# Gated delta rule of a two-part block: chunks of 128 tokens in place of 64, with waits for one token tile

## The chip, the cores and the metric

The kernel runs as one program on one core of one Trainium2 chip. The metric is the device time of one execution in microseconds (us). TensorE is called PE below, VectorE DVE, ScalarE ACT, GpSimd POOL and SyncE SP.

## The reference

The reference computes two small models in a row on 256 tokens of width 1024, all in float32. The first has two layers; its second layer is the gated delta rule, which the change is about. The second model has two layers of mixing and an expert layer each (16 experts, three 1024 x 1024 matrices per expert).

```
def gated_delta_rule(q, k, v, g, beta):
    c = DN_CHUNK                                   # 64
...
    g = jnp.cumsum(g, axis=-1)                     # within a chunk
    decay = jnp.exp(jnp.where(tril, g[..., :, None] - g[..., None, :], -jnp.inf))
    m = jnp.where(strict, jnp.einsum('bhncd,bhnsd->bhncs', kb, k) * decay, 0.0)
    t_inv = lax.linalg.triangular_solve(eye + m, ...)
    u = t_inv @ vb
    w = t_inv @ (kb * jnp.exp(g)[..., None])
    qk = jnp.where(tril, jnp.einsum('bhncd,bhnsd->bhncs', q, k) * decay, 0.0)

    def step(state, xs):
        v_new = u_c - w_c @ state
        o = (q_c * jnp.exp(g_c)[..., None]) @ state + qk_c @ v_new
...
        state = state * jnp.exp(g_last)[..., None, None] + jnp.einsum('bhcd,bhce->bhde', k_dec, v_new)
        return state, o
```

There are 8 heads of 128. The result is a recurrence over tokens, and the chunk length is only a way to compute it: a longer chunk gives the same output.

## The kernel before

All weights come from HBM in pieces of up to 2 MB that SP's queue moves into a ring of three slots. The order of the pieces is the order in which PE first uses them, and a piece is asked for when the slot that it needs is free. Weights of the ordinary layers are then split by ACT (`act_hi`, tile m_WH) and DVE (`dve_lo`, tile m_WL) into two parts, in units of 1024 columns, two units ahead of PE.

The order on each engine is the order in which the Python functions are called, `pe_program`, `act_program` and `dve_program`. The delta rule lies in `pe_odd`, `act_odd` and `dve_odd`; each has an inner `mix(H)` for heads 0 to 3 (H = 0) and 4 to 7 (H = 1). Token tiles t = 0 and 1 are 128 tokens each. The steps of `mix` are: transposes of K and V; column sums for the norm of q; the decay matrices; products k k^T and q k^T (`kk`), scaled on DVE and transposed (`kkT`); then the inverse of the triangular matrix by levels. A level l takes three steps: DVE masks the matrix (`B`), PE multiplies it with T (`BT`, 8 products), ACT copies the result out (`Y`), PE multiplies again (`TTY`, up to 16 products), and DVE subtracts. Level 0 needs no product and levels 1 to 5 give the inverse of blocks of 64. Then come U and w, and the recurrence over four chunks of 64 tokens, `for n in range(4)`. At the end the output is normed, multiplied with the gate z and transposed (`OT`).

Between the steps stand calls `pe_jobs.fill(n)`, and the same on ACT and DVE. A fill takes the next n pieces from a queue of other work: projections for the second half of the heads (24 products of 256 columns for a piece, or 12 of 512 for z), then the output projection of the first half. DVE also does a convolution (`conv`) for every second piece of a projection to q, k or v. When that queue is empty, a fill takes a piece from the idle job `pe_ada`, here called an ada piece: it belongs to the second model. There are 24; each needs one 2 MB transfer into the ring, 8 products of 512 columns on PE (tile m_ring by m_misc), a copy on ACT to m_adaT, 4 transposes and two sums on DVE. `pe_jobs.finish()` empties the queue, though not the idle job. Where fills have not used up the idle job, `run(pe_jobs.idle)` runs the rest in one go, between `pe_ple(1)` and `pe_mixer(0)`, and ACT and DVE do the same. In the kernel before nothing is left by then.

## Time and profile before

| | us |
|---|---|
| median of 3 runs (lowest, highest) | 2462.76 (2462.62, 2471.58) |
| the profiled execution | 2464.88 |
| its span in the trace | 2463.6 |
| PE busy | 1940.9 (79% of the span) |
| DVE busy | 956.6 (39%) |
| ACT busy | 711.2 (29%) |
| mean granted clock of PE, full = 1 | 0.906 |

The page cuts the span in 40 slices of 61.6 us. The delta rule lies in slices 8 to 13 (461 to 826 us from the start), the end of `pe_ple(1)` at 1100 us in slice 17, and the expert layers, in which the transfers run without a break, in slices 22 to 28 and 32 to 39. The median of the runs and the profiled execution differ by 2 us.

### The profile page before, as it was taken

To read this page: it belongs to the slowest core of one execution; us is meant where nothing else is said; L and a number is where in the kernel's file an instruction comes from. 1 tells how busy PE (TensorE), PEld (TensorE's weight loads), DVE (VectorE), ACT (ScalarE), POOL (GpSimd) and SP (SyncE) were. 2 spreads that over 40 slices of the span, in tenths; PEclk is the share of its full clock that TensorE was granted. 3 is DMA by queue.
4 is the path that set the end of the run, shared out by engine and by line. 5 is a ranking of instruction groups with operands and counts; after the bars stand their busy time and mean duration, and the time that the engine had idled before them with its cause. 6 is when DMAs were issued, how large, how long until landed. Compare 5 with 4: busy or idle time off the path is not lost.

```text
span 2463.6 us, 30239 instructions
## 1 busy us (share of the span) xinstructions
PE 1940.9 (79%) x13272; PEld 1380.4 (56%) x13272; DVE 956.6 (39%) x1724; ACT 711.2 (29%) x1150; POOL 4.1 (0%) x11
## 2 busy tenths in 40 slices
PE   6788997788888699968895888888868856666666
PEld 5687997677565599957673332333236632323223
DVE  6765556665443555475446010101054520001010
ACT  4444444563232344453433100000033410000000
POOL 0000000000000000000000000000000000000000
PEclk9899998998999799989997999999988977878788
DMA  5234353422658254530121999999953359999998
GB/s 231 103 137 171 138 194 128 171 103 72 249 214 321 84 189 156 200 121 26 69 108 64 400 430 430 430 430 428 431 236 120 123 225 430 429 430 430 430 429 339
DMA packets 44788, 606.47 MB, mean 246 GB/s; under 512 B 5105, under 2 KB 5233, under 8 KB 6769
## 3 DMA queue, kind: packets, MB, share of 16 engines
q1 hardware_dynamic: 43488, 597.61, 60.0%
q0 software_dynamic: 880, 4.98, 0.6%
q8 instruction: 104, 1.70, 0.3%
q10 hardware_dynamic: 288, 1.95, 0.2%
q14 instruction: 28, 0.22, 0.0%
HBM read 603.47 MB, written 1.05 MB: 245 GB/s over the span
## 4 chain that ended last, share of the span: by engine, by line
PE 50%; DMA 25%; DVE 16%; ACT 6%; issue 2%; SPq 0%; DVEq 0%; POOLq 0%; ACTq 0%
PE ps L85 48%; DMA m_last_slot<-moe_down 15%; DMA m_more<-moe_up 9%; PE ps L88 2%; DVE m_WL L94 2%; DVE m_od L94 2%; DVE m_od L100 2%; ACT m_WH L91 1%; ACT m_mix_sc L91 1%; DVE m_misc L103 1%; DVE m_wk L100 1%; DVE m_misc L112 1%; DVE m_wk L94 1%; ACT m_od L91 1%; DMA m_praw<-pT 1%
## 5 line engine op out<-in xcount | busy, mean ns | idle before, releaser
L85 PE MATMUL ps<-m_ring,m_moe_sc 128*32 128x256 f32 (+1 forms) x2304 | 414.2, 545 | 79.9 <-DMA m_ring<-moe_gate 74.8
L94 DVE TENSOR_TENSOR m_WL<-m_ring,m_WH 128x1024 fp32r<-128x1024 f32 (+1 forms) x277 | 331.5, 1203 | 309.3 <-ACT m_WH L91 308.9
L91 ACT ACTIVATE m_WH<-m_ring 128x1024 fp32r<-128x1024 f32 (+1 forms) x277 | 284.8, 1035 | 160.3 <-PE ps L85 155.6
L85 PE MATMUL ps<-m_nH,m_WH 128*128 128x256 f32 x1136 | 294.6, 295 | 16.6 <-ACT m_WH L91 13.2
L85 PE MATMUL ps<-m_nL,m_WH 128*128 128x256 f32 x1136 | 291.3, 292 | 1.6 <-DVE m_nL L94 1.6
L85 PEld LDWEIGHTS ps<-m_ring,m_moe_sc 128*32 128x32 f32 (+1 forms) x2304 | 154.2, 143 | 230.0 <-issue 123.3
L85 PE MATMUL ps<-m_more,m_moe_sc 128*32 128x256 f32 (+1 forms) x768 | 204.7, 546 | 78.4 <-DMA m_more<-moe_up 78.4
L85 PEld LDWEIGHTS ps<-m_nH,m_WH 128*128 128x128 f32 x1136 | 226.8, 200 | 23.0 <-ACT m_WH L91 15.4
L94 DVE TENSOR_TENSOR m_nT<-ps,m_nT 128x512 f32<-128x512 f32 (+1 forms) x32 | 17.9, 558 | 546.2 <-PE ps L85 546.2
L85 PEld LDWEIGHTS ps<-m_nL,m_WH 128*128 128x128 f32 x1136 | 226.7, 200 | 4.2 <-DVE m_nL L94 3.9
L85 PE MATMUL ps<-m_last_slot,m_nT 128*32 128x256 f32 (+1 forms) x768 | 189.1, 507 | 32.5 <-DMA m_last_slot<-moe_down 32.5
L91 ACT ACTIVATE m_nT<-ps 128x512 f32<-128x512 f32 (+1 forms) x64 | 31.4, 491 | 610.6 <-PE ps L88 315.1
L85 PE MATMUL ps<-m_more,m_nT 128*32 128x256 f32 (+1 forms) x768 | 192.0, 507 | 18.5 <-ACT m_nT L91 18.5
L85 PEld LDWEIGHTS ps<-m_more,m_moe_sc 128*32 128x32 f32 (+1 forms) x768 | 72.7, 144 | 184.5 <-DMA m_more<-moe_up 95.9
L85 PE MATMUL ps<-m_nH,m_WL 128*128 128x256 f32 x1136 | 160.9, 285 | 0.0
L85 PEld LDWEIGHTS ps<-m_nH,m_WL 128*128 128x128 f32 x1136 | 148.5, 194 | 0.0
L106 DVE COPY m_moe_sc<-ps 32x256 f32<-32x256 f32 (+3 forms) x62 | 32.9, 530 | 297.4 <-PE ps L85 296.3
L91 ACT ACTIVATE m_moe_sc<-ps 32x256 f32<-32x256 f32 (+2 forms) x66 | 32.3, 489 | 290.2 <-PE ps L85 255.6
L85 PEld LDWEIGHTS ps<-m_more,m_nT 128*32 128x32 f32 (+1 forms) x768 | 66.4, 133 | 83.5 <-issue 56.2
L85 PE MATMUL ps<-m_od 128*128 128x128 f32 (+2 forms) x672 | 94.2, 299 | 19.6 <-DVE m_od L94 19.4
L85 PEld LDWEIGHTS ps<-m_last_slot,m_nT 128*32 128x32 f32 (+1 forms) x768 | 67.9, 133 | 72.4 <-DMA m_last_slot<-moe_down 42.3
L85 PEld LDWEIGHTS ps<-m_od 128*128 128x128 f32 (+2 forms) x672 | 87.8, 206 | 26.4 <-DVE m_od L94 20.8
(270 smaller groups left out, 2827.2 us busy)
## 6 DMA issues: line engine op xcount, KB each, us to landing
m_ring<-moe_gate SPq DMA_DIRECT2D x64, 2048.0 KB, 18.8
m_ring<-moe_up SPq DMA_DIRECT2D x32, 2048.0 KB, 17.2
m_more<-moe_up SPq DMA_DIRECT2D x32, 2048.0 KB, 21.7
m_more<-moe_down SPq DMA_DIRECT2D x32, 2048.0 KB, 17.6
m_last_slot<-moe_down SPq DMA_DIRECT2D x32, 2048.0 KB, 22.1
m_ring<-ada SPq DMA_DIRECT2D x24, 2048.0 KB, 7.8
m_ring<-ffn_down SPq DMA_DIRECT2D x16, 1408.0 KB, 6.0
m_ring<-ffn_gate SPq DMA_DIRECT2D x10, 2048.0 KB, 7.8
```

Source lines behind the costliest of these rows:

```text
L85: return Issued() if self.dry else self.e.matmul(out, lhsT, rhs, start=start, stop=stop, skip_group_check=skip)
L88: return Issued() if self.dry else self.e.transpose(*a)
L91: return Issued() if self.dry else self.e.activation(*a, **k)
L94: return Issued() if self.dry else self.e.tensor_tensor(*a)
L100: return Issued() if self.dry else self.e.scalar_tensor_tensor(*a)
L103: return Issued() if self.dry else self.e.tensor_reduce(*a)
L106: return Issued() if self.dry else self.e.tensor_copy(*a)
L112: return Issued() if self.dry else self.e.reciprocal(*a)
```

## The change

The chunk is 128 tokens long, one token tile, in place of 64.

- The inverse takes levels 1 to 6 in place of 1 to 5. The last level of both has only the product for TT.
- The recurrence has two chunks. The first has no state before it, the second has no state after it: what is left is `kv` and `o` of tile 0 and `wS`, `qS` and `o` of tile 1, and `w` is computed for tile 1 only. The products are of full 128 rows.
- Events of the inverse are kept for each token tile: B, TT0, "T out" and "TT out" of tile t are waited for, not those of both. DVE works on 512 columns at a time in place of 1024.
- In `mix`, both decay matrices come before the transposes of K, and the products `kk` of both tiles come before their transposes.
- On DVE the next mask comes before the subtractions of the level before; there is one fill in a level in place of two; fewer fills stand in the recurrence.
- The gate sums are taken from the middle of the chunk, by three small products with constant matrices at once. The norm at the end and z are applied per tile.
- The constants grow by 128 columns, and a scratch tile shrinks.

```diff
-    ("rcos", 256), ("rsin", 256), ("levels", 768), ("cumT", 128), ("lastT", 128),
-    ("sel", 256), ("dmask", 128),
+    ("rcos", 256), ("rsin", 256), ("levels", 896), ("cumT", 128), ("tailT", 128),
+    ("fullT", 128), ("spare", 128), ("dmask", 128),
...
-            ps, before = fg.take("cum", "gcu")
+            ps, before = fg.take("cum", "cum read")
             pe.wait_ge(*before).wait_ge(*at("g"))
-            pe.matmul(ps[:, 0:16], sm("cumT"), gcu, True, True).then_inc(*P.mark("cum"))
+            for i, what in enumerate(("cumT", "fullT", "tailT")):
+                ins = pe.matmul(ps[:, 16 * i:16 * i + 16], sm(what), decays, True, True)
+            ins.then_inc(*P.mark("cum"))
             pe_jobs.fill(1)
-            ps, before = fg.take("last", "EL")
...
                     ps, before = fg.take(("decay", H, t), ("decay out", H, t))
                     pe.wait_ge(*before).wait_ge(*at(("diag", H, t)))
-                    pe.matmul(ps[:, :], ones, Y[:, 0:512], True, False)
+                    pe.matmul(ps[:, :], ones, Y[:, t * 512:(t + 1) * 512], True, False)
                     pe.matmul(ps[:, :].rearrange("p (h t) -> p h t", h=4), ident, bc(sm("dmask").unsqueeze(1), [128, 4, 128]), False, True).then_inc(
...
-                    for kind in range(2):
+                for t in range(2):
+                    pe_transposes(("knT", H, t), [K[:, t * 512 + h * 128:t * 512 + (h + 1) * 128] for h in range(4)], [("kn", H)], fg, ("knT out", H, t))
+                pe_jobs.fill(1)
+                for kind in range(2):
+                    for t in range(2):
...
-                        if kind == 0:
-                            pe_jobs.fill(1)
-                        pe_transposes(("kkT", H, t, kind), [vT[:, h * 128:(h + 1) * 128] for h in range(4)], [("kk read", H, t, kind)],
-                                      fg, ("kkT out", H, t, kind))
+                    pe_jobs.fill(1)
+                    for t in range(2):
+                        pe_transposes(("kkT", H, t, kind), [vT[:, t * 512 + h * 128:t * 512 + (h + 1) * 128] for h in range(4)],
+                                      [("kk read", H, t, kind)], fg, ("kkT out", H, t, kind))
...
-                for t in range(2):
-                    pe_transposes(("TT", H, t), [TT[:, t * 512 + h * 128:t * 512 + (h + 1) * 128] for h in range(4)], [("TT0", H)], fg, ("T out", H, 0, t))
-                for l in range(1, 6):
+                for t in range(2):
+                    pe_transposes(("TT", H, t), [TT[:, t * 512 + h * 128:t * 512 + (h + 1) * 128] for h in range(4)], [("TT0", H, t)], fg, ("T out", H, 0, t))
+                for l in range(1, 7):
                     for t in range(2):
                         ps, before = fg.take(("BT", H, l, t), ("Y", H, l, t))
-                        pe.wait_ge(*before).wait_ge(*at(("B", H, l))).wait_ge(*at(("T out", H, l - 1, 1)))
-                        if l > 1:
...
-                            pe.wait_ge(*before).wait_ge(*at(("Y", H, l, 1)))
+                            pe.wait_ge(*before).wait_ge(*at(("Y", H, l, t)))
+                            if l > 1:
+                                pe.wait_ge(*at(("TT out", H, l - 1, t)))
...
-                    pe_jobs.fill(1)
                 U, wT, vn = Vv, kbg, Y
-                for t in range(2):
...
+                for what, t in (("U", 0), ("w", 1), ("U", 1)):
+                    ps, before = fg.take((what, H, t), (what + " out", H, t))
+                    pe.wait_ge(*before).wait_ge(*at(("TT out", H, 6, t)))
...
+                for what, t in (("kv", 0), ("o", 0), ("wS", 1), ("qS", 1), ("o", 1)):
+                    read, ready = {"kv": ("St", ("U out", H, 0)), "o": ("O copy", ("U out", H, 0) if t == 0 else ("vn", H)),
+                                   "wS": ("vn", ("w out", H, 1)), "qS": ("qS out", ("St", H))}[what]
+                    read = (read, H, t) if what == "o" else (read, H)
+                    if what == "wS":
+                        pe_jobs.fill(1)
+                    if what == "o" and t:
+                        pe_jobs.fill(1)
+                    ps, before = fg.take((what, H, t), read)
+                    pe.wait_ge(*before).wait_ge(*at(ready))
+                    if what == "wS":
+                        pe.wait_ge(*at(("St", H)))
...
-                for n in range(4):
-                    t, o = n // 2, 64 * (n % 2)
-                    r = slice(o, o + 64)
-                    if n:
...
-                pe_jobs.fill(2)
-                for t in range(2):
...
+                    pe_transposes(("OT", H, t), [T[:, t * 512 + h * 128:t * 512 + (h + 1) * 128] for h in range(4)], [("Oz", H, t)], fg, ("oL", H, t))
...
-                            act.wait_ge(*at(("TTY", H, l - 1, 1)))
+                            act.wait_ge(*at(("TTY", H, l - 1, t)))
                         act_copy(Y[:, t * 512:(t + 1) * 512], bank["BT", H, l, t][:, :], [("BT", H, l, t)], ("Y", H, l, t))
-                    act_jobs.fill(2)
-                for t in range(2):
...
+                act_copy(T[:, 0:512], bank["o", H, 0][:, :], [("o", H, 0)], ("O copy", H, 0))
+                act_jobs.fill(1)
+
+                def norm(t):
+                    half = slice(t * 512, (t + 1) * 512)
+                    act_squares(("O", H, t), T[:, half].rearrange("p (h d) -> p h d", h=4), BT[:, half].rearrange("p (h d) -> p h d", h=4),
+                                [("O copy", H, 0) if t == 0 else ("O copy", H, 1)])
+                    act_power(("O", H, t), o_rk[:, 4 * t:4 * t + 4])
+                norm(0)
+                act.wait_ge(*at(("qS", H, 1)))
+                for h in range(4):
+                    act.activation(T[:, 512 + h * 128:640 + h * 128], bank["qS", H, 1][:, h * 128:(h + 1) * 128], ACT.Copy,
+                                   scale=o_rq2[:, 4 + h:5 + h]).then_inc(*A.mark(("qS out", H)))
+                act_jobs.fill(1)
+                norm(1)
+                for t in range(2):
...
+            def subtract(H, what, l, t):
+                T, TT = (S(i) for i in rest[H][5:7])
+                d = (T if what == "T" else TT)[:, t * 512:(t + 1) * 512]
+                dve.wait_ge(*at((what + "Y", H, l, t)))
+                dve.tensor_tensor(d, d, bank[what + "Y", H, l, t][:, :], ALU.subtract).then_inc(*V.mark((what + " out", H, l, t)))
...
+                scaled = [(Vv, Vv, beta, 0), (Vv, Vv, beta, 1), (kbg, K, be, 1), (K, K, kd_, 0)]
+                for l in range(1, 7):
+                    for t in range(2):
+                        if l > 1:
+                            dve.wait_ge(*at(("BT", H, l - 1, t)))
+                        dve.wait_ge(*V.now()).tensor_tensor(d4t(BT, t), d4t(MT, t), lv(l), ALU.mult).then_inc(*V.mark(("B", H, l, t)))
+                    if l > 1:
+                        for t in range(2):
+                            for what in ("T", "TT"):
+                                subtract(H, what, l - 1, t)
+                    if l <= 4:
+                        dst, a, by, t = scaled[l - 1]
...
+                    dve_jobs.fill(1)
+                for t in range(2):
+                    subtract(H, "TT", 6, t)
+                z3 = z.rearrange("p (h d) -> p h d", h=8)
+                dve.wait_ge(*at(("z", H, 1)))
+                dve.tensor_tensor(z3, z3, bc(sm("o_g").unsqueeze(1), [128, 8, 128]), ALU.mult).then_inc(*V.mark())
+                dve.wait_ge(*at(("kv", H, 0)))
+                dve.tensor_copy(St, bank["kv", H, 0][:, :]).then_inc(*V.mark(("St", H)))
...
+                def norm(t):
+                    half = slice(t * 512, (t + 1) * 512)
+                    dve_mean_square(("O", H, t), BT[:, half].rearrange("p (h d) -> p h d", h=4), o_rk[:, 4 * t:4 * t + 4], 128)
+                    dve.wait_ge(*at(("power", ("O", H, t))))
+                    for h in range(4):
+                        o = slice(t * 512 + h * 128, t * 512 + (h + 1) * 128)
+                        dve.scalar_tensor_tensor(T[:, o], T[:, o], o_rk[:, 4 * t + h:4 * t + h + 1], z[:, o], ALU.mult, ALU.mult).then_inc(
+                            *V.mark(("Oz", H, t)))
+                dve.wait_ge(*at(("wS", H, 1))).wait_ge(*at(("U out", H, 1)))
+                dve.tensor_tensor(Y[:, 512:1024], Vv[:, 512:1024], bank["wS", H, 1][:, :], ALU.subtract).then_inc(*V.mark(("vn", H)))
+                norm(0)
+                dve_jobs.fill(1)
+                dve.wait_ge(*at(("o", H, 1))).wait_ge(*at(("qS out", H)))
+                dve.tensor_tensor(T[:, 512:1024], T[:, 512:1024], bank["o", H, 1][:, :], ALU.add).then_inc(*V.mark(("O copy", H, 1)))
+                norm(1)
...
-    for l in range(6):
+    for l in range(7):
...
-    same = (i[:, None] // 64) == (i[None, :] // 64)
-    c["cumT"] = (same & (i[:, None] <= i[None, :])).astype(f)
-    c["lastT"] = (same & (i[:, None] % 64 == 63)).astype(f)
-    c["sel"] = np.concatenate([np.tile((i == 63 + 64 * j).astype(f)[:, None], (1, 128)) for j in range(2)], 1)
-    c["dmask"] = np.where(same & (i[None, :] <= i[:, None]), 0.0, BIG).astype(f)
+    to = (i[:, None] <= i[None, :]).astype(f)
+    c["cumT"] = np.where(i[None, :] >= 64, to * (i[:, None] >= 64), (to - 1) * (i[:, None] < 64)).astype(f)
+    c["tailT"] = 1 - to
+    c["fullT"] = to
+    c["spare"] = np.zeros((128, 128), f)
+    c["dmask"] = np.where(i[None, :] <= i[:, None], 0.0, BIG).astype(f)
...
```

The first place is PE in the inverse of heads 4 to 7: one level and the start of the next. The products m_od by m_od are BT and TTY, m_ring by m_misc with its transposes is one ada piece. Before:

```order
L85 MATMUL ps<-m_od 128x128 x8
L85 MATMUL ps<-m_ring,m_misc 32x512 x8
L88 MATMUL ps<-m_small,m_adaT 128x128 x4
L85 MATMUL ps<-m_od 128x128 x16
L85 MATMUL ps<-m_ring,m_misc 32x512 x8
L88 MATMUL ps<-m_small,m_adaT 128x128 x4
L85 MATMUL ps<-m_od 128x128 x8
```

And now, at the same place:

```order
L88 MATMUL ps<-m_small,m_od 128x128 x16
L85 MATMUL ps<-m_od 128x128 x8
L85 MATMUL ps<-m_ring,m_misc 32x512 x8
L88 MATMUL ps<-m_small,m_adaT 128x128 x4
L85 MATMUL ps<-m_od 128x128 x24
L85 MATMUL ps<-m_ring,m_misc 32x512 x8
L88 MATMUL ps<-m_small,m_adaT 128x128 x4
```

The 16 products of a level and the 8 of the next now stand together, with one ada piece in a level in place of two.

The second place is PE between the last gate weights of `pe_ple(1)` (m_nH by m_WL) and the first product of `pe_mixer(0)` (m_WH by m_m2H). Before:

```order
L85 MATMUL ps<-m_nL,m_WH 128x256
L85 MATMUL ps<-m_nH,m_WL 128x256 x8
L85 MATMUL ps<-m_small 128x256 x2
L85 MATMUL ps<-m_wk,m_small 128x256 x2
L85 MATMUL ps<-m_WH,m_m2H 128x512
```

And now; the first two of the added rows stand there nine times, of which one is shown:

```order
L85 MATMUL ps<-m_nH,m_WL 128x256 x8
L85 MATMUL ps<-m_ring,m_misc 32x512 x8
L88 MATMUL ps<-m_small,m_adaT 128x128 x4
...
L85 MATMUL ps<-m_ring,m_misc 32x512 x8
L88 MATMUL ps<-m_small,m_adaT 128x128 x8
L85 MATMUL ps<-m_small 128x256 x2
L85 MATMUL ps<-m_wk,m_small 128x256 x2
L85 MATMUL ps<-m_WH,m_m2H 128x512
```

Ten ada pieces have moved from the fills of `pe_odd` to the run of what is left of the idle job. On ACT the two splits of the first mixer weights, which stood among the last steps of `act_ple(1)`, now stand behind its ten copies to m_adaT:

```order
L91 ACTIVATE m_wk<-m_xT 128x512
L91 ACTIVATE m_adaT<-ps 128x512 x10
L91 ACTIVATE m_WH<-m_ring 128x1024 x2
L91 ACT_TABLE_LOAD
L91 ACTIVATE m_misc<-m_small 128x1
L91 ACTIVATE m_small<-ps,m_small 128x256
```

## Rows read from the trace of the kernel before

**Rows 1.** Page, part 2: GB/s moved in each of 40 slices of the span.

```profile
GB/s 231 103 137 171 138 194 128 171 103 72 249 214 321 84 189 156 200 121 26 69 108 64 400 430 430 430 430 428 431 236 120 123 225 430 429 430 430 430 429 339
```

**Rows 2.** Windows of the delta rule: from:to length, busy us by engine, PEclk, DMA, GB/s.

```profile
515.60:564.00 48.40, 38.32 (x238) 33.04 (x236) 27.36 (x56) 28.79 (x45) 0.00 (x0) 0.92 0.30 114
564.00:642.50 78.50, 68.38 (x516) 63.31 (x517) 39.52 (x67) 27.59 (x43) 0.00 (x0) 0.92 0.25 90
642.50:673.80 31.30, 25.38 (x188) 14.11 (x188) 14.32 (x39) 7.31 (x11) 0.00 (x0) 0.93 0.78 289
673.80:721.60 47.80, 37.92 (x268) 29.52 (x268) 24.54 (x62) 19.55 (x34) 0.00 (x0) 0.93 0.57 219
721.60:784.90 63.30, 55.64 (x408) 38.58 (x412) 22.91 (x54) 11.34 (x19) 0.00 (x0) 0.87 0.78 284
784.90:796.30 11.40, 10.56 (x89) 7.03 (x88) 2.65 (x9) 4.17 (x7) 0.00 (x0) 1.00 0.96 382
796.30:828.20 31.90, 18.34 (x120) 13.79 (x120) 15.17 (x37) 7.05 (x11) 0.00 (x0) 0.76 0.30 117
```

**Rows 3.** Waits of PE, 515 to 829 us: us in total, times, longest.

```profile
PE ps L85 <- DVE m_od L94: 19.4, 12, 2.7
PE ps L88 <- DVE m_od L94: 18.3, 6, 8.1
```

**Rows 4.** PE timeline, one level of H = 1: start, us, instructions, idle before.

```profile
736.75 2.97 PE L85 MATMUL ps<-m_od 128*128 128x128 f32 x16 [1.90 <-DVE m_od L94]
...
742.16 0.66 PE L88 MATMUL ps<-m_small,m_adaT 128*128 128x128 f32 x4
742.65 3.74 PE L85 MATMUL ps<-m_od 128*128 128x128 f32 x32
746.32 1.93 PE L85 MATMUL ps<-m_ring,m_misc 128*32 128x512 f32 x16
748.17 0.66 PE L88 MATMUL ps<-m_small,m_adaT 128*128 128x128 f32 x4
```

**Rows 5.** PE timeline, start of H = 0.

```profile
515.67 1.91 PE L88 MATMUL ps<-m_small,m_od 128*128 128x128 f32 x16
517.34 0.36 PE L85 MATMUL ps<-m_nH,m_WH 128*128 128x256 f32 x1
...
520.46 1.92 PE L85 MATMUL ps<-m_small,m_od 128*128 128x1 f32 x16
```

**Rows 6.** DVE timeline, a level of H = 0.

```profile
584.00 2.71 DVE L100 SCALAR_TENSOR_TENSOR m_od<-m_wk,m_small,m_od 128x256 f32<-128x256 f32 x6 [1.64 <-ACT m_od L91]
586.63 2.48 DVE L94 TENSOR_TENSOR m_od<-m_od,ps 128x512 f32<-128x512 f32 x4
...
590.15 1.22 DVE L94 TENSOR_TENSOR m_od<-m_od,m_small 128x1024 f32<-128x1024 f32 x1
```

**Rows 7.** Chain of waits, end of H = 1: start, us, what.

```profile
816.64 1.18 DVE m_od L100 x4
...
824.67 1.98 PE ps L88 x8
```

**Rows 8.** Transfers of ada pieces, 600 to 800 us: count, KB each, us to landing.

```profile
m_ring<-ada SPq DMA_DIRECT2D x20, 2048.0 KB, 7.8
```

**Rows 9.** SP queue's timeline, 1083 to 1103 us.

```profile
1083.11 11.00 SPq L124 DMA_DIRECT2D m_ring<-w_in  x2
```

**Rows 10.** Transfers of the whole execution, POOL's queue.

```profile
m_mix_sc<-dft POOLq DMA_DIRECT2D x2, 640.0 KB, 4.1
```

**Rows 11.** ACT timeline, end of the last gate of the first model.

```profile
1095.66 1.99 ACT L91 ACTIVATE m_WH<-m_ring 128x1024 fp32r<-128x1024 f32 x2
```

**Rows 12.** Chain of waits into the first mixer.

```profile
1101.10 1.28 ACT L91
...
1102.99 1.75 DVE m_small L112
...
1115.04 34.96 PE ps L85 x143
```

More of the change, by code:

```diff
@@ L265, in program @@
         wk = sb("wk", 2048)
-        misc = sb("misc", 1152)
+        misc = sb("misc", 1056)
         adaT = sb("adaT", 512)
@@ L1350, in mix @@
-                pe_jobs.fill(2)
-                for t in range(2):
-                    pe_transposes(("OT", H, t), [T[:, t * 512 + h * 128:t * 512 + (h + 1) * 128] for h in range(4)], [("Oz", H)], fg, ("oL", H, t))
+                        if what == "U":
+                            ins = pe.matmul(ps[:, h * 128:(h + 1) * 128], p8(TT)[:, i, :], p8(Vv)[:, i, :], True, True)
+                        else:
+                            ins = pe.matmul(ps[:, h * 128:(h + 1) * 128], p8(kbg)[:, i, :], p8(TT)[:, i, :], True, True)
@@ L1459, in mix @@
-                act_squares(("O", H), T.rearrange("p (h d) -> p h d", h=8), BT.rearrange("p (h d) -> p h d", h=8), [("O", H, 3), ("O copy", H, 3)])
-                act_power(("O", H), o_rk)
-                act_jobs.fill(2)
-                for t in range(2):
+                    act_jobs.fill(1)
+                for what, t in (("U", 0), ("w", 1), ("U", 1)):
+                    act_copy((Vv if what == "U" else kbg)[:, t * 512:(t + 1) * 512], bank[what, H, t][:, :], [(what, H, t)], (what + " out", H, t))
@@ L1549, in mix @@
[L1549 to L1555 removed]
+                dve_jobs.fill(2)
+                for kind in range(2):
+                    for t in range(2):
@@ L1625, in mix @@
-                dve_jobs.fill(2)
-                for t in range(2):
+                d4t = lambda a, t: a[:, t * 512:(t + 1) * 512].rearrange("p (i t) -> p i t", i=4)
+                lv = lambda l: bc(sm("levels", 128 * l, 128 * l + 128).unsqueeze(1), [128, 4, 128])
+                for t in range(2):
+                    dve.wait_ge(*at(("kkT out", H, t, 0))).tensor_tensor(d4t(BT, t), d4t(MT, t), lv(0), ALU.mult).then_inc(*V.mark())
+                    dve.wait_ge(*V.now()).tensor_tensor(d4t(TT, t), bc(ident.unsqueeze(1), [128, 4, 128]), d4t(BT, t), ALU.subtract).then_inc(
+                        *V.mark(("TT0", H, t)))
@@ L1627, in mix @@
+                for t in range(2):
+                    dve_jobs.fill(1)
                     dve_parts(oL[:, 4 * H:4 * H + 4, t * 128:(t + 1) * 128], bank["OT", H, t][:, :].rearrange("p (k t) -> p k t", k=4),
```

188 lines of the change are left out of this document (44 added, 144 removed).

## The prediction

> **What bounds the kernel now.** I read the slices first. From slice 22 to 28 and from 32 to 39 the core moves 430 GB/s without a break: the expert weights are the bound there, and the change touches nothing of them [rows 1]. Ahead of that the rate is 21 to 321 GB/s, so transfers are not the bound, and a microsecond saved there moves all that follows forward by one, since the ring of three slots cannot fetch the expert weights much earlier. The question is what the delta rule costs. The windows put it at 312.6 us, from the first transposes of H = 0 to the first output product of H = 1, and in that time PE is busy 254.5 us; DVE and ACT at most 60% of any window [rows 2]. So it is PE and the chains that PE waits for. The list of waits says that PE stands idle 38 us for DVE results in m_od alone [rows 3]. The timeline shows the second part of the loss: after a wait of 1.9 us, 16 product rows (two for one fp32 product) take 2.97 us, while 32 take 3.74 otherwise [rows 4]. The granted clock is 0.87 in the levels of H = 1 and 0.76 in its recurrence [rows 2], so part of "busy" is half speed, 1.2 for 2.4 GHz, behind a wait.
>
> **How much of the 312.6 us is work.** Unit costs at full clock: a product 128x128x128 0.234 us (3.74 / 16) and an ada piece 2.34 (1.85 from row to row, and 0.49 for the transposes) [rows 4]; a transpose 0.104 (1.67 / 16), the column sums 1.8, and a projection piece 3.12 (24 products in the time from 517.34 to 520.46) [rows 5]; a z piece as much, its columns are the same in number. For H = 0 the program has 56 transposes (5.8), column sums (1.8), four wide decay products at 4 x 0.234 (3.7), 16 + 112 + 68 = 196 products for kk, levels and recurrence (45.9), 12 + 4 projection pieces (49.9) and 7 ada pieces (16.4): 123.5. For H = 1 it is the same with 4 output pieces (12.5) and 15.5 ada pieces (36.3): 106.0. Together 229.5. The other 83 us are waits and half speed.
>
> **What the change takes from the work.** The level that is added has 24 products, the recurrence and U/w fall from 68 to 32: 12 fewer for each half, 24 x 0.234 = 5.6 us. Of the 22 ada pieces in the two halves 11 stay: 11 x 2.34 = 25.7 us gone from here. Together 31.3 us, on the engine that bounds the stage.
>
> **What happens to the 83 us.** In a level of H = 1 PE now has 8 + 16 products and one ada piece, 5.6 + 2.3 = 8.0 us. What must be late for PE to wait? T of tile 0 is ready for its subtraction after 4 products (0.9 us), and the subtraction takes 0.62 [rows 6]; ahead of it DVE has two masks of about 0.6 each (half of 1.22) and the sums of the ada piece, together 2 us after the level's second product begins. So it is done at 2.6, and PE needs it at 3.7. I cost the wait at nothing: the other tile's products hide it. DVE has about 6 us of work in 8. Against 63.3 us for five levels [rows 2] six take 5 x 8.0 + 6.1 = 46. What I expect to stay, in us:
> - H = 0 up to the first level 6: kk still waits for the copy of knT behind a convolution, and TT0 and the first mask stand in a row at its end.
> - Levels of H = 0: 5. One convolution, 2.71 [rows 6], now falls between a projection piece and the subtraction of T with only 3.7 us of products over it, and the clock falls once.
> - End of H = 0: 9. The last convolution and its silu come after the last projection piece, and the transposes of V of H = 1 wait for them. Before, ada pieces stood there as cover: this is a new wait.
> - H = 1 up to its first level 7, its levels 2, its end 5: the norm of tile 1 alone stands after the last product, and then copy and split. Before, the norm took 8.0 us from 816.64 to 824.67 [rows 7]; by halves of all operations it is about 5, and one ada piece lies over it.
>
> That is 34 of 83 us, so 49 are saved. Bounds: if the waits move rather than go, as little as 15; if all that I listed is hidden too, 65. I take 49, since levels and recurrence, where I see the cover instruction by instruction, hold most of the 83. Stage: 31 + 49 = 80 us less (46 to 96).
>
> By the Trainium skill ("TensorE: Matmul & The Clock Gate", "What's actually happening") half rate is the default and sustained activity releases it, and "A second HAM failure mode" warns that short idles between product groups are enough to make the clock swing. The rows at 0.87 and the 2.97 us [rows 2, 4] agree. If the clock stays at 0.87 in the new levels, twelve levels of some 8 us cost 14 us more; that is rival C.
>
> **What the change adds.** One of the 11 ada pieces goes to the start of the next feed-forward stage, where PE waits for a norm: nothing. Ten go between the first model and the first mixer, and there they are alone on the path. PE needs 2.34 us for each, a transfer of 2.097 MB at 430 GB/s needs 4.88 [rows 1, 8], so the transfers set the pace. Three ada pieces take the place of the three mixer pieces that were fetched early; the last is asked for at 1083.11 + 11.00 = 1094.1 [rows 9] and lands 7.8 us later [rows 8], at 1101.9 in times of before. Then seven more and the first mixer piece follow: 8 x 4.88 = 39.0, at 1140.9. A 640 KB transfer on POOL's queue falls into the same time and shares the 430 GB/s: 1.5 [rows 10]. Then ACT makes the two splits that used to be done early, 1.99 [rows 11]. From its table load to the reciprocal is 1.89 (1101.10 to 1102.99), and from there to the first mixer product 12.05 (to 1115.04) [rows 12]: 1158.3, against 1115.04. Cost 43 us. Bounds: PE alone, 10 x 2.34 = 23; every transfer after the other with its whole 7.8 us, 8 x 7.8 in place of 39.0: 66. I take 43, as three slots keep two transfers waiting at any time. At half clock PE would need 4.7 us for a piece, still within 4.88.
>
> By the Trainium skill ("DMA: Bandwidth & Descriptors", "Where 436 GB/s comes from") about 358 GB/s of HBM per core should bind. The trace does not agree: 430 for hundreds of microseconds [rows 1]. By the page's figure the eight transfers would take 47 us and the tail 51.
>
> **The sum.** -31 - 49 + 43 = -37 us. The gate sums, the constants (64 KB more in a load at the start, under other work), and the start of the stage I cost at nothing; the expert layers keep their length. The profiled execution took 2464.9 us: 2428. The runs' median is 2 us lower: 2426.
>
> **Rivals.**
> A, the forecast: -20 to -55 us, 2426, chance 0.62.
> B, more: PE without a gap in both halves, only 18 us of loss left, as the cover above hints, -96 + 40 = -56: 2407. For it: the products of a tile cover all short chains. Against it: every stage of this trace keeps some waits. 0.17.
> C, the clock: waits become shorter and more frequent, and the granted clock stays at 0.87 in the levels: -37 + 14 = -23: 2440. 0.05.
> D, the waits move: DVE works in order, convolutions and weight splits stand ahead of the subtractions, and half of what I save comes back as waits for them: stage -55, tail +43, -12: 2451, on the edge of what can be seen. Against it: DVE is at half load [rows 2]. 0.12.
> E, slower: the ten ada pieces run one after the other, each waiting for a transfer asked for only when its slot is free, its copy and its transposes. With 7.8 us from issue to landing [rows 8], and products and transposes at half clock, 3.7 and 1.0, a step takes 12.5 us and not 4.88. Eight take 100, the tail costs 104, and with 80 saved that is +24: 2487. A step of 9.5 us makes the change worth nothing, and from 11 us on it is slower by what can be measured. Against it: three slots. 0.04.
>
> **How the numbers follow.** This kernel's measurement can tell about 0.5% (12 us) from no change. Faster by more: A, B, C and half of D, 0.90; within: the other half of D, 0.06; slower: E, 0.04. The range takes A and B's and C's centres and stops short of D: 2404 to 2448.
>
> **What would show it.** After: the delta rule some 80 us shorter; a level of H = 1 at 8 us without a wait on m_od and a clock near 1; m_od by m_od products 24 in a row. Between the last gate of the first model and the first mixer product a stretch of 430 GB/s, about 40 us longer, with ten copies to m_adaT 4.9 us apart. Wrong if a level is over 10 us, if PE waits for the convolution in most levels of H = 0, or if the copies to m_adaT lie 9 us or more apart.

## The result, and the profile after

The kernel after takes 2433.8 us (median of 4 runs, 2432.3 to 2436.4) against 2466.4 (4 runs, 2462.6 to 2471.6): a ratio of 0.987, with a 95% interval of 0.984 to 0.989. In a later set of runs it is 2433.2 against 2469.6, 0.986 (0.984 to 0.988). The change is an improvement of 1.3 to 1.4%. The prediction was 2426, within 2404 to 2448, and of the mechanisms A.

The profiled execution took 2434.6 us, its span is 2433.2, against 2463.6: 30.4 us less, where 37 were forecast. To see where they come from, I follow the same work through both traces by its start times.

| | before | after | difference | forecast |
|---|---|---|---|---|
| start of the span to the first transposes of H = 0 | 515.6 | 516.4 | +0.8 | 0 |
| delta rule, first transposes of H = 0 to first output product of H = 1 | 312.6 | 227.7 | -84.9 | -80 |
| from there to the last product of the second feed-forward stage | 217.6 | 215.2 | -2.4 | 0 |
| from there to the first mixer product, with ten ada pieces | 68.3 | 116.2 | +47.9 | +43 |
| from there to the end of the span | 1349.5 | 1357.7 | +8.2 | 0 |
| sum | | | -30.4 | -37 |

The slices of the page, GB/s, answer to [rows 1]. The levels of H = 1 with their ada pieces lie in the slice of 243 (669 to 730 us); the next one, 274, also holds the output weights and the first feed-forward weights. What matters more is that the full slices of the expert layers read 427 to 429 where they read 428 to 431 before:

```profile
GB/s 234 96 136 167 157 184 133 147 139 70 70 243 274 194 155 197 191 256 74 1 173 116 428 427 429 428 428 427 428 167 104 139 270 427 427 428 427 427 428 327
```

The windows of the delta rule answer to [rows 2]. Each row has from:to and length, then the busy us of PE, PEld (PE's weight loads), DVE, ACT and POOL with their instructions, the granted clock, the DMA share and GB/s. The stretches are the start of H = 0, its six levels, its end, the start of H = 1, its six levels, its end:

```profile
516.45:557.06 40.61, 33.42 (x213) 29.17 (x212) 23.82 (x55) 24.59 (x41) 0.00 (x0) 0.88 0.22 86
557.06:609.70 52.64, 49.52 (x382) 47.62 (x381) 33.18 (x48) 16.68 (x25) 0.00 (x0) 0.97 0.23 81
609.70:643.70 34.00, 23.52 (x198) 22.87 (x197) 23.14 (x44) 19.49 (x34) 0.00 (x0) 0.93 0.18 62
643.70:676.20 32.50, 30.34 (x212) 26.16 (x212) 16.66 (x45) 14.91 (x27) 0.00 (x0) 0.91 0.24 82
676.20:722.85 46.65, 45.86 (x398) 36.20 (x397) 26.94 (x56) 11.94 (x20) 0.00 (x0) 1.00 0.74 266
722.85:744.15 21.30, 18.01 (x153) 11.49 (x152) 11.16 (x34) 10.62 (x21) 0.00 (x0) 1.00 0.84 333
```

Six levels of H = 1 take 46.7 us at a clock of 1.00, where five took 63.3 at 0.87. PE is busy 200.7 of 227.7 us in the stage, so it stands idle for 27 us, against 58 before (312.6 less 254.5). The chain of waits shows that a level is PE alone (start, us, what), and where the half ends:

```profile
697.74 7.21 PE ps L85 x64
704.95 0.59 PE ps L88 x4
705.54 7.21 PE ps L85 x64
712.75 0.59 PE ps L88 x4
...
733.69 9.34 DMA m_ring<-od_out
743.02 0.02 issue
743.04 1.06 ACT m_WH L91
```

That answers to [rows 4]. A level takes 7.80 us: 64 rows of products (48 of the level's 24 products, two for each, and 16 of the ada piece) and 4 transposes, with no wait among them. The end is another matter. The output weights of the second half are asked for only at 733.69 and land at 743.0. PE's timeline says what that costs, 3.29 us in front of the first output product:

```profile
740.26 0.60 PE L88 MATMUL ps<-m_small,m_od 128*128 128x128 f32 x4
744.15 0.39 PE L85 MATMUL ps<-m_oH,m_WH 128*128 128x256 f32 x1 [3.29 <-ACT m_WH L91]
```

The waits of PE in m_od, 516 to 760 us, answer to [rows 3]; the waits for DVE of 19.4 and 18.3 us have become 3.3 and 4.3, and a wait for ACT of 8.4 stands at the end of H = 0, where the last convolution and its silu are waited for:

```profile
PE ps L88 <- ACT m_od L91: 8.4, 1, 8.4
PE ps L88 <- DVE m_od L94: 4.3, 4, 2.4
PE ps L85 <- DVE m_od L94: 3.3, 2, 3.0
```

The tail answers to [rows 9 and 12]. The chain of waits runs over every third transfer of an ada piece. Such a transfer is asked for when a slot comes free and lands 12.7 to 13 us later:

```profile
1027.13 12.97 DMA m_ring<-ada
1040.11 0.04 issue
1040.15 1.97 PE ps L85 x16
1042.12 0.02 issue
1042.13 12.67 DMA m_ring<-ada
...
1054.84 3.03 PE ps L85 x16
...
1076.48 3.68 PE ps L85 x9
```

From the piece at 1024.09 to that at 1054.84 are six steps, 5.1 us each. Over the whole execution the ada transfers land after 8.2 us (median). Here three are in flight, so each lands 13 us after its request, and still one lands every 5 us.

### The profile page after: what moved, and what is told of

Read it like the earlier page. It is cut to its first block, busy times and chain, and to the rows that moved or that the text cites. A ratio compares the mean times of both kernels' runs of the same rounds, so it can differ in the third digit from the quotient of the medians.

```text
span 2433.2 us, 30159 instructions
## 1 busy us (share of the span) xinstructions
PE 1919.7 (79%) x13222; PEld 1371.9 (56%) x13222; DVE 949.6 (39%) x1719; ACT 709.6 (29%) x1157; POOL 4.1 (0%) x11
## 4 chain that ended last, share of the span: by engine, by line
PE 50%; DMA 28%; DVE 14%; ACT 6%; issue 2%; SPq 0%; DVEq 0%; POOLq 0%; ACTq 0%
PE ps L85 48%; DMA m_last_slot<-moe_down 15%; DMA m_more<-moe_up 9%; DVE m_WL L94 2%; PE ps L88 2%; ACT m_WH L91 1%; DMA m_ring<-ada 1%; ACT m_mix_sc L91 1%; DVE m_od L100 1%; DVE m_misc L103 1%; DVE m_wk L100 1%; DVE m_misc L112 1%; ACT m_od L91 1%; DVE m_wk L94 1%; DMA m_praw<-pT 1%
## 5 line engine op out<-in xcount | busy, mean ns | idle before, releaser
L85 PE MATMUL ps<-m_nH,m_WH 128*128 128x256 f32 x1136 | 291.2, 292 | 14.9 <-ACT m_WH L91 14.8
L85 PE MATMUL ps<-m_more,m_moe_sc 128*32 128x256 f32 (+1 forms) x768 | 210.2, 562 | 85.3 <-DMA m_more<-moe_up 85.3
L85 PE MATMUL ps<-m_last_slot,m_nT 128*32 128x256 f32 (+1 forms) x768 | 187.8, 503 | 30.4 <-DMA m_last_slot<-moe_down 30.4
L85 PE MATMUL ps<-m_od 128*128 128x128 f32 x688 | 84.4, 283 | 6.5 <-DVE m_od L94 3.3
L85 PEld LDWEIGHTS ps<-m_od 128*128 128x128 f32 x688 | 82.1, 198 | 7.9 <-DVE m_od L94 4.0
```

Source lines behind the costliest of these rows:

```text
L85: return Issued() if self.dry else self.e.matmul(out, lhsT, rhs, start=start, stop=stop, skip_group_check=skip)
```

## The experiments

The time between SP's request for the first w_four weights and the end of the span serves below as a measure for the second model. It begins some 10 us behind the first mixer's first product and holds both expert layers. It is 1338.4 us before (2463.6 less 1125.19) and 1347.5 after.

**The kernel after, once more.** No edit.

> The kernel after, once more, on the chip of the three runs beside it: 2434 us (2432 to 2437). Its trace tells whether the seven us that the gain lost inside the expert layers belong to the kernel. If they do, the first product of the first expert layer stands some 1115 to 1116 us before the end of the span again, as it did (1115.3), and not 1108 as in the trace before. If they are a matter of the single execution, it moves by some us while everything ahead of it stays in place.

Measured: 2433.2 us, span 2430.5. The w_four request stands at 1085.06 (1085.72 in the first trace) and the rest is 1345.4 us. The expert layers read 426 to 429 GB/s. By the mark of the expectation, the first product of the first expert layer stands 1115.2 us before the end (2430.5 less 1315.3), as in the first trace (1115.3), and not 1108.2 as in the kernel before. By both marks the loss of some 7 us is there again, so it is no matter of a single execution. By the request for w_four the two traces of this kernel differ by 2 us.

**The ten pieces of the tail moved into the feed-forward stages.**

```
 run(pe_dense((tag, "up", j0), "ffn_up", (l,), js, 8, ...))
+pe_jobs.fill(SPOTS[l].count((j0, 1)))      # 6 in the first FFN, 4 in the second; ACT and DVE alike
```

> The kernel after with the ten ada pieces of the tail moved into the two FFN stages, one behind the up products of each group of four tiles (six in the first FFN, four in the second). Theory, that the tail costs some 47 us because ten pieces wait there for one 2 MB transfer each, while the FFN leaves the transfers half idle: the tail goes (-47), ten pieces of 2.34 us are paid on PE in its place (+23), so 2410 us, 2406 to 2416. Rival 1, that the pieces in the FFN hold a ring slot back and so delay the weights behind them: up to 4.9 us more for each, 2434 to 2445. Rival 2, that the transfers of the expert layers' stage set the end whatever comes before: no change, 2430 to 2436.

Measured: 2414.5 us (2410.0 to 2417.1), 19 less than the kernel after. "The tail" is here the run of the ten ada pieces. SP's requests for ple_gate and w_four enclose it and show both terms. After, and in this kernel:

```profile
947.79 6.94 SPq L124 DMA_DIRECT2D m_ring<-ple_gate  x2
...
1085.72 25.37 SPq L124 DMA_DIRECT2D m_ring<-w_four  x2
```

```profile
974.22 6.94 SPq L125 DMA_DIRECT2D m_ring<-ple_gate  x2
...
1065.01 25.38 SPq L125 DMA_DIRECT2D m_ring<-w_four  x2
```

The stretch is 137.9 us with the pieces and 90.8 without (90.9 in the kernel before): the tail costs 47.1 us. In the feed-forward stages the pieces push ple_gate back by 26.4, 2.6 us each. In the first feed-forward stage, 205.56 to 382 us, PE is busy without a gap at full clock and the transfers take 64% of the time, so the ring keeps up:

```profile
205.56:382.00 176.44, 176.44 (x1472) 167.02 (x1470) 88.19 (x100) 75.03 (x88) 0.00 (x0) 1.00 0.64 233
```

The time lies in the range of the theory, and neither rival's price shows.

**Small transfers in the tail.**

```
+if name == "ada" and n >= W.whole[14]:
+    width = 512                              # 256 KB in place of 2 MB
```

> The kernel after, but each of the ten ada pieces of the tail moves 256 KB in place of 2 MB and multiplies what lies in the ring otherwise, so the output is not the reference's. Theory, that the transfers set the pace of the tail (4.9 us a piece): PE, ACT and DVE alone need 1.9 for the products, 0.6 for the copy and 0.6 for the transposes, one behind the other for each piece with some waits, 3.2 to 3.6 us apart, and the first of the ten starts without its wait of 3.5 us: the tail is 15 to 22 us shorter, 2415 us, 2411 to 2420. Rival, that the chain of PE and ACT sets it: no change, 2431 to 2436.

Measured: 2408.8 us (2407.6 to 2413.3), 24 less than after, so the transfers set the pace of the tail. The gain is larger than I expected (15 to 22): without them a piece takes 2.44 us, not 3.2 to 3.6, since ACT's copy hides under the next piece's products.

```profile
1014.34 1.92 PE L85 MATMUL ps<-m_ring,m_misc 128*32 128x512 f32 x16
1016.19 0.66 PE L88 MATMUL ps<-m_small,m_adaT 128*128 128x128 f32 x4
1016.78 1.92 PE L85 MATMUL ps<-m_ring,m_misc 128*32 128x512 f32 x16
```

The stretch from ple_gate to w_four is 112.2 us here: of the 47.1, 25.7 go with the large transfers, and 21.4 are left for the ten pieces.

**A second fill in the levels of H = 1.** The kernel before has two fills in a level, after has one; does the tail come back into the levels at their PE price?

```
 # PE, at the end of level l
+pe_jobs.fill(H)
 # ACT: act_jobs.fill(1)  ->  act_jobs.fill(1 + H)
 # DVE: dve_jobs.fill(1)  ->  dve_jobs.fill(1 + H)
```

> The kernel after with a second fill in each level of H = 1, as before the change: six more ada pieces run there, four are left in the tail. Theory: each level grows by one piece, from 7.80 to 10.1 us (+14), since two transfers of 4.9 us just fit into it, and the tail loses six transfers (-29): 2419 us, 2414 to 2424. Rival 1, that the transfers don't keep up and PE waits for each second piece, so that the levels cost what the tail saves: 2430 to 2436. Rival 2, that a fill in a level is free because it stands in a wait: then the levels stay near 7.8 to 8.5 us and the time is 2405 to 2410.

Measured: 2439.4 us (2438.7 to 2440.8), six more than after; all three guesses were wrong. A level took 13.5 to 16 us. The transfers aren't it: PE waits for none of them in these levels, and for DVE five times 2.60 us. DVE's timeline shows the sums of the second piece at 703.21, when its transposes are done, and the masks and subtractions of the level only behind them, at 703.71 and 705.05. PE has stood since 703.2 and goes on at 705.78:

```profile
702.52 0.66 PE L88 MATMUL ps<-m_small,m_adaT 128*128 128x128 f32 x4
703.21 0.26 DVE L103 TENSOR_REDUCE m_misc<-ps 128x4 f32<-128x16 f32 x2 [5.55 <-PE ps L88]
703.51 0.17 DVE L94 TENSOR_TENSOR m_misc<-m_misc,m_small 128x8 f32<-128x8 f32 x1
703.71 1.42 DVE L94 TENSOR_TENSOR m_od<-m_od,m_small 128x512 f32<-128x512 f32 x2
705.05 2.47 DVE L94 TENSOR_TENSOR m_od<-m_od,ps 128x512 f32<-128x512 f32 x4
705.78 3.65 PE L85 MATMUL ps<-m_od 128*128 128x128 f32 x16 [2.60 <-DVE m_od L94]
```

The clock has a part in it as well. The 16 rows behind the wait take 3.65 us where 32 take 3.74 at full clock [rows 4], and the granted clock of four of these levels is 0.81 to 0.97.

I had put the second fill of DVE in one call with the first, ahead of the masks of the next level. So I moved it on DVE alone:

```
 for t in range(2):
     for what in ("T", "TT"):
         subtract(H, what, l - 1, t)
+dve_jobs.fill(H)                             # and dve_jobs.fill(1) behind it as in the kernel after
```

> The kernel after with the second fill in each level of H = 1 once more, but on DVE it stands behind the subtractions of the level before, as it does in the kernel before the change, and no longer in one call with the first. In the run with both in one call a level took 14.7 us in place of 10.1. Theory, that DVE's sums of the second piece, which PE transposes only behind the second products of the level, stood ahead of DVE's masks of the next level and so put the whole DVE chain on the path: with the other place on DVE alone the level takes 10.1 to 10.6 us, the stage is 14 to 17 us longer than in the kernel after, the tail 31 us shorter: 2419 us, 2414 to 2424. Rival, that PE waits for the transfer of each second piece (two of 4.9 us in a level): the levels stay at 12 to 15 us and the time at 2430 to 2440.

Measured: 2420.6 us (2418.5 to 2423.3), as the theory had it. The same pieces are on the same engines; only one group of operations stands in another place of DVE's order, and that is worth 19 us (the two ran on different chips, where the kernel before takes 2469.6 and 2470.8). A level is now 10.24 us, with PE without a gap and a granted clock of 1.00, and the two transfers fit just inside it. Of the 4.6 us more of a level before (14.8 on average over four), 2.6 were the wait; PE's busy time made up the rest, 12.2 us in place of 10.24 for the same rows.

```profile
690.75 5.43 PE ps L85 x48
696.18 0.59 PE ps L88 x4
696.77 3.64 PE ps L85 x32
700.41 0.59 PE ps L88 x4
700.99 5.43 PE ps L85 x48
```

The tail with four pieces takes 107.5 us from ple_gate to w_four: 16.7 for four pieces and 30.4 for the six beyond them (5.1 each). The first pieces of a tail are the cheaper ones: in the kernel after PE starts the first three at 1013.21, 1015.65 and 1018.09, 2.44 us apart and without a wait.

**Waits for both tiles in the levels.**

```
-pe.wait_ge(*at(("B", H, l, t))).wait_ge(*at(("T out", H, l - 1, t)))
+pe.wait_ge(*at(("B", H, l, 1))).wait_ge(*at(("T out", H, l - 1, 1)))   # Y and TT out alike
```

> The kernel after, but in the six levels each product waits for both token tiles, as before the change; nothing else differs. Theory, that the waits for one tile bring little: by the trace of after the last T of a level is subtracted at 685.87 while PE is ready for BT at 685.66, so 0.2 to 0.5 us come back in each of the ten later levels, and a little more in the levels of H = 0, where DVE also convolves: +3 to +8 us, 2437 to 2442. Rival, that the waits for one tile carry most of the 49 us of waits that went: +15 to +40 us, 2449 to 2474.

Measured: 2443.0 us (2437.7 to 2447.0), 10 more. Only PE waits for both tiles here; ACT and DVE still work tile by tile, in the new order. In H = 1 the level is 8.35 us in place of 7.80. PE stands 0.32 us in front of each level's first products, and the rest lies between the rows next to that wait:

```profile
693.36 2.02 PE L85 MATMUL ps<-m_od 128*128 128x128 f32 x16 [0.32 <-DVE m_od L94]
...
697.66 3.74 PE L85 MATMUL ps<-m_od 128*128 128x128 f32 x32
701.71 0.46 PE L85 MATMUL ps<-m_od 128*128 128x128 f32 x2 [0.32 <-DVE m_od L94]
```

By the start times of the same work H = 0 is 6.4 us longer and H = 1 is 3.7. In H = 0 the wait of PE at the convolution is 4.28 us in place of 2.99. The whole is a little over my +3 to +8 and far from the rival's +15. So of some 53 us of waits that the stage lost beside its 31 of work, PE's waits by tile hold 10. Where the other 43 went is not shown: the shorter recurrence, the masks ahead of the subtractions, and the halves of U, w and the norm changed with them, and no run takes these apart.

**One level fewer.**

```
-for l in range(1, 7):
+for l in range(1, 6):      # the fill of the sixth level is kept
```

> The kernel after without its sixth level (the inverse is then that of the two blocks of 64 alone, so the output is not the reference's); the fills are all kept. It prices the level that the change adds, for each half of the heads. Theory: the level costs its PE time alone, 7.80 less the ada piece of 2.5 in H = 1, and 8.1 less the projection piece of 2.9 in H = 0, so -5.2 to -5.3 each and 2423 us, 2420 to 2425. Rival, that the level's DVE and ACT chain is on the path too, as two or three us of wait each: 2416 to 2420. Rival 2, that the end of H = 1 waits for the output weights whatever the levels take: -5 in all, 2428.

Measured: 2421.9 us (2420.3 to 2424.4), 11.3 less than after. In the trace the stage is 10.5 us shorter, 5.2 for each half, as the theory had it: a level costs what its 24 products take on PE, and no wait of its own. So the added level is 10 to 11 us of the stage, which is 84.9 shorter all the same.

**The output weights earlier.** To the kernel with the ada pieces in the feed-forward stages:

```
-pe_jobs.fill(1)            # the four fills of H = 1 behind the levels
+pe_jobs.fill(1 - H)        # ACT and DVE alike; 8 and 6 pieces in the two FFN stages
```

> The kernel with the ada pieces in the FFN stages, and also without the four ada pieces at the end of H = 1, which move to the FFN stages too (eight in the first, six in the second, one after the other as before). Theory, that these four keep the ring's slots and so put off the request for the output weights of the second half, whose transfer then ends 3.3 us after PE is ready: the request stands 10 us or more earlier against PE, the wait goes, the number of pieces paid on PE is the same: 2411 us, 2408 to 2414, against 2414.5. Rival, that the four pieces filled waits of the recurrence and cost there less than the 2.4 to 2.8 us of a piece in the FFN: 2414 to 2419.

Measured: 2414.1 us (2413.5 to 2418.4) against 2414.5: no gain. The request did move, to 722.51, and the transfer is no longer waited for. But PE now waits for the norm and the copies, which the four pieces had covered:

```profile
749.64 0.63 PE L89 MATMUL ps<-m_small,m_od 128*128 128x128 f32 x4 [1.55 <-DVE m_od L101]
753.41 1.11 PE L89 MATMUL ps<-m_small,m_od 128*128 128x128 f32 x4 [3.14 <-DVE m_od L101]
756.16 0.58 PE L86 MATMUL ps<-m_oH,m_WH 128*128 128x256 f32 x1 [1.63 <-ACT m_WH L92]
```

These are 6.3 us where the kernel with ten pieces moved waits 2.84 for the split of these weights. The wait for the transfer lay beside a chain of nearly the same length, so it was worth little by itself. The time lies on the border of the two ranges; the waits speak for the rival.

**Two pieces at the starts of stages.** As the last, with one more piece at the start of the delta rule layer and of the second feed-forward stage, and two fewer behind feed-forward products:

```
 pe_stats(tag, acc[0], [("ss", before, 0, 6)])
-pe_jobs.fill(1)
+pe_jobs.fill(1 + l)        # on ACT both ahead of act_norm
```

> As the run with the output weights early, but one more ada piece stands at the start of the delta rule layer and one more at the start of the second FFN, where PE waits for the norm anyway (on ACT both copies stand ahead of the norm), and two fewer behind FFN products. Theory: a piece there costs 0 to 0.6 us in place of 2.4, so 4 us less than with the output weights early: 2407 us, 2403 to 2411. Rival, that the ada weights in the ring put off the first weights of the stage, by one transfer of 4.9 us each, or that ACT's copies delay the norm: no gain or up to +8, 2411 to 2420.

Measured: 2424.0 us (2421.2 to 2431.6), 10 more than with the output weights early, and worse than the rival's +8. The first mechanism of the rival is what the trace shows (it is the slowest of the four executions, 2431.6 us). The two pieces and the output weights fill the three slots, so that the first feed-forward weights are asked for at 768.15, when the output weights are split, and not at 738.11. ACT stands in front of the split of these weights, and the squares that the norm needs are behind it in ACT's order. At the norm PE waits 11.62 us where it waited 4.24 with the output weights early:

```profile
766.89 1.24 DVE m_WL L95
768.13 0.02 issue
768.15 8.78 DMA m_ring<-ffn_gate
776.93 0.02 issue
776.95 1.06 ACT m_WH L92
```

**The kernel before, and its table padded.** Two runs ask where the slower expert layers come from. The first has no edit, the second only this:

```
-"small": asc(small),
+"small": asc(cat([small, np.zeros((128, 128), small.dtype)], 1)),
```

> The kernel before, profiled once more. From the request of the first w_four weights to the end of the span (the second model behind its first mixer's start) the trace before took 1338.4 us, the six traces of kernels with the change 1345.1 to 1348.3, with 430 against 427 to 428 GB/s in the expert layers. If that is a matter of the single execution, this trace takes 1338 to 1348; if it belongs to the kernel, 1338 to 1340 again.

> The kernel before with 128 unused columns more in the input table of constants, 64 KB as the change adds them, which moves every array behind it in HBM; no instruction differs. Theory, that the slower expert layers of the kernels with the change come from where the weights now lie: from the first w_four request to the end 1345 to 1348 us in place of 1338.4, 427 to 428 GB/s, and the time 5 to 8 us longer than the kernel before beside it. Rival, that the place is nothing to it: 1338 to 1340 us or the spread of the kernel before, and the same time.

Measured: the kernel before again takes 2471.7 us (2460.0 to 2474.6, 8 runs) and has 1339.4 us from w_four to the end (2465.1 less 1125.74) and 429 to 431 GB/s in the full slices. With the padded table it is 2468.6 us (2461.5 to 2472.9, 10 runs), 1338.1 us and 429 to 430 GB/s; the time is the same as that of the kernel before beside it (ratio 1.001, 0.999 to 1.002). So the slower layers belong to the change and not to the place of the weights in HBM. My theory fell. The padded kernel ran on the same chip as the one with small tail transfers, which reads 426 to 429, so it isn't the chip either.

**The ring at its old SBUF address.** What is left of the change in the second model is where the tiles lie: m_small grew by 512 bytes in each partition and m_misc shrank by 384, so the ring begins at byte 64448 of each partition, not at 64320, and all behind it too. To the kernel with the pieces in the feed-forward stages:

```
-misc = sb("misc", 1056)
+misc = sb("misc", 1024)
-ea, gt, o_rq, ... = mi(8), mi(48), mi(8), ...
+ea, gt, o_rq, ... = mi(8), sm("spare", 0, 48), mi(8), ...
```

> The kernel with the ada pieces in the FFN stages (2414.5 us), and with its small tile m_misc 32 columns shorter, so that the ring and every tile behind it lie at the same SBUF addresses as in the kernel before; in the kernels with the change they lie 128 bytes further. Theory, that the slower expert layers come from the address that the weights are written to in SBUF: from the first w_four request to the end 1338 to 1341 us in place of 1348, 430 GB/s in place of 427 to 428, and 2407 us, 2403 to 2411. Rival, that it is something else of the change: 1345 to 1348 us and 427 to 428 GB/s again, 2411 to 2417.

Measured: 2405.9 us (2403.2 to 2407.0, 5 runs), ratio to the kernel before 0.974 (0.971 to 0.977). From w_four to the end it takes 1340.8 us (2404.7 less 1063.88) against the 1348.3 of the same kernel with the ring at its new place, and the rate is back:

```profile
GB/s 237 81 144 197 245 226 199 105 150 71 71 181 292 239 217 191 129 103 75 35 140 160 430 430 430 430 430 430 430 146 105 141 282 430 430 429 429 429 430 340
```

The theory holds: 128 bytes of address cost 7.5 us in this pair of traces. (The mean of the ten traces with the new addresses is 7.4 us above that of the four with the old.) It is also the best version that I found, 28 us faster than the kernel after and 61 faster than the kernel before.

## Why the prediction was right, and where it was off

*The work removed, -31.* The count is right: PE's instructions in the seven windows before are 1827 and in the six after 1556, which is 271 fewer, and 24 products of two rows and 11 ada pieces of 20 make 268. PE's busy time in the stage fell by more, by 53.8 us, from 254.5 to 200.7. The other 22 us I put down to rows at half speed before, since the clock in the levels of H = 1 rose from 0.87 to 1.00; no run takes them apart.

*The waits, -49.* With half speed counted in, as in the prediction, this is -53.6 (84.9 less 31.3), and 29.5 us are left of the 34 that I listed. By PE's idle time in the windows, the start of H = 0 was forecast at 6 us and is 7.2; its levels at 5 and are 3.1, nearly all one stall of 2.99 at the convolution; its end at 9 and is 10.5, with one wait of 8.36; the start of H = 1 at 7 and is 2.2, and its levels at 2 and are 0.8, ahead of the first products. So the largest miss in the list is the start of H = 1, 5 us too much. For the end of H = 1 I had the norm of tile 1, 5 us. It is 3.3, but by the transfer of the output weights, which I had not seen: I counted a fill as 2.34 us of PE and forgot that its slot in the ring is taken from the next weights. The run without these fills shows that without them the norm and the copies take as much or more (6.3 us).

*The level of 8 us.* It is 7.80, at a clock of 1.00. DVE is busy for 4.9 of it, less than the 6 I had reckoned. Rival C is out: PE has no gap in these levels, and the clock stays up. Even the waits of 0.32 us with both tiles, one in each level of 8.35 us, did not bring it down: 32 rows of products take 3.74 us there, and the granted clock over five levels (686.96 to 728.73) is 1.00. The Trainium skill ("TensorE: Matmul & The Clock Gate", "A second HAM failure mode") says that short, frequent idles between groups of products are enough to make the clock swing. With a gap of 0.32 us in every level this case does not show it. With gaps of 1.9 us before the change [rows 4], and of 2.6 us with the second fill in one call, it does.

*The ada pieces, +43.* This term was too small: it is 47.1 by the experiment, 47.9 in the traces. The mechanism is shown: three in flight, paced by the transfers. Of the 4 to 5 us that were missing, 1.5 are the step, 5.13 us and not 4.88, over six steps; 1.9 are POOL's 256 KB transfer for the gated embedding in the same stretch, which stands behind three ada pieces and takes 9.15 us where it took 7.28. The remaining 1 us I did not trace. Rival E had every transfer alone on the path, 12.5 us a step. Landing times are indeed 12.7 to 13 us, but the transfers overlap.

*The expert layers, 0.* This was the worst of the terms: +8.2. "The expert layers keep their length" is the step that failed. I had looked at the 64 KB more to load, and not at where the larger table pushes the ring, which costs 7.5 us.

*The sum.* That it came within 7 us of -37 is in part luck. The stage gained 5 us more than forecast and the ada pieces cost 5 more, which cancels; what is left of the error is the 8.2 us of the expert layers less 1.6 us gained just ahead of and behind the delta rule.

*A reading.* The prediction gives 21 to 321 GB/s ahead of the expert layers; the lowest value of [rows 1] is 26. Nothing hangs on it.

*Rivals B and D.* B had 18 us of loss left in the stage, and there are 29.5; the end of H = 0 alone holds 8.4. D did not come with this change, but the second fill in one call is of its kind: DVE's order put sums ahead of masks, and that cost 19 us.

## What to carry to other kernels

Work that is used as cover is not gone when the waits that it covered are gone: count where the rest of it runs, and whether there it is paid by the engine (2.4 to 2.6 us for a piece here) or by its transfer (5.1 us). Put it where PE is busy and the transfers are not, a place that looks worst by PE's share of busy time. And when a constant or a scratch tile changes its size, look at the SBUF addresses behind it as well: if a stretch bound by transfers changes its rate by half a percent, try the old address before any other theory.

## What the runs showed of the hardware

- The rate of the 2 MB transfers depends on the SBUF address. With the ring at byte 64320 four traces read 428 to 431 GB/s in their full slices and take 1338.1 to 1340.8 us from the w_four request to the end; with all tiles 128 bytes further ten traces read 426 to 429 and take 1344.8 to 1348.3. Which property of the address it is stays open.
- An obvious candidate does not fit. Half of the expert transfers go to the ring and half to m_more and m_last_slot, which lie behind it. By the offsets in the kernels the ring starts 64 bytes behind a multiple of 256 before and 192 behind one after; the other two start at a multiple before and 128 behind one after. The Trainium skill ("DMA: Bandwidth & Descriptors", "How a descriptor splits into AXI transactions") says that a transaction must start at a multiple of 256 bytes, so that a descriptor that starts in between also pays the beats of 32 bytes ahead of it; it speaks of reading. If writing were the same, a row of 16 KB (2 MB over 128 partitions, 512 beats) would take 514 beats in the ring before and 518 after, and 512 and 516 in the other two: an estimate of 0.8% more for both. Measured are 430 to 427.5 GB/s, 0.6%, and 7.5 us in some 940 of full transfers, 0.8%. But by the same rule a row to the ring would be 0.4% or 2.4 ns longer than one to the other two, and the trace does not agree: in the second expert layer a row takes 612.8 to 613.4 ns to the ring and 612.4 to 612.8 to the others in the four traces with the old addresses, and 615.3 to 615.8 and 614.9 to 616.1 in the ten with the new ones. No run here has the ring at a multiple of 256.
- The place in HBM shows in the latency alone, if at all: the eight od_in transfers of 2 MB land after 7.6 us (median) in both traces of the kernel before, after 8.0 with the padded table and 8.0 in the best version, while the rate stays at 430.
- The kernel before spreads over 2460 to 2479 us in its runs, and the kernels with the change over 2 to 10. In one set its shortest run (2464.1 us) has a mean granted clock of 0.909 and its longest (2472.0 us) 0.902; no run here shows what decides it.
